# Summing the modulations over partitions inside the preceding stage, with GpSimd held back until the norm is over

## The chip, the cores and the metric

One core of one Trainium2 chip runs the whole program. The metric is device time in microseconds (us) of one execution. Three runs of the kernel before gave 4388.53, 4393.25 and 4394.18 us; the median is 4393.25.

## The reference, cut to what matters

Two transformer blocks of different make, each two layers deep, act on x (256 tokens, width 1024, fp32). In order there are ten sections, each with its own adaptive norm in front and gate behind:

```python
for l in range(2):                                  # first block: sections 0 to 5
    m = (silu(c) @ w_mod[l] + b_mod[l]).reshape(3, 3, D)
    x = x + 0.5 * m[0, 2] * swiglu(adaln_in(x, norm_g[l, 0], m, 0), ...)       # ffn, width 2752
    x = x + m[1, 2] * (mix(adaln_in(x, norm_g[l, 1], m, 1) @ w_in[l]) @ w_out[l])  # attention + conv
    x = x + 0.5 * m[2, 2] * swiglu(adaln_in(x, norm_g[l, 2], m, 2), ...)
for l in range(2):                                  # second block: sections 6 to 9
    sh_m, sc_m, g_m, sh_f, sc_f, g_f = split(silu(c_2) @ w_mod_2[l] + b_mod_2[l], 6)
    x = x + g_m * mixer(rms_norm(x, g) * (1 + sc_m) + sh_m, ...)               # three branches
    x = x + g_f * moe_ffn(rms_norm(x, g) * (1 + sc_f) + sh_f, ...)             # 64 experts, top 8
# adaln_in(x, g, m, i) = rmsnorm(x, g) * (1 + m[i, 1]) + m[i, 0]
```

A section needs a modulation of three vectors of 1024: shift, scale and gate. Each is a vector times a 1024 x 1024 part of `w_mod`. It depends on c alone, not on x, so it can be made at any time ahead.

## The kernel before, in words

The five engines run five hand-written streams, ordered by semaphores. x and h are kept transposed, as 8 tiles of 128 channels x 256 tokens. The sections are, by number: 0 ffn, 1 mixer "ab", 2 ffn, 3 ffn, 4 mixer "cd", 5 ffn, 6 "mix2", 7 moe, 8 "mix2", 9 moe. "Norm s" below is the norm in front of section s.

**Sections.** An ffn or moe section (`units`) goes through units of 256 hidden columns: 1 rest unit and 10 full ones for ffn, 1 shared expert and 64 experts for moe. Each product is three fp32r matmuls, for which ACT makes the rounded half of each weight (`split_up`, `split_down`) and DVE the remainder (`lo_up`, `lo_down`); DVE also makes the hidden values (`hidden`). The units run in a loop of `two_units`, and the last pair stands behind the loop. In a moe section the router (L1017 on TensorE, L1902 on DVE) comes first; its gates are turned by TensorE (`turn_gates`, L1027, L1030) and copied by DVE (L1946, `gates_turned`). A mixer section projects h (`linear`, L802), does attention and convolutions with much small work on DVE, and ends with four output projections and the addition to x (L1549). `next_halves` prepares the first weight halves of the next ffn during the tail of a mixer.

**The norm.** ACT squares x (L1117); TensorE adds the squares over partitions with eight matmuls against ones (L712, bank 2); ACT takes the root (L1124) and DVE the reciprocal (L1518). DVE makes h = x * gain * rstd for eight tiles (L1525); ACT adds the shift (`h_ready`). For ffn, DVE makes the remainder h_lo after each (`lo_h`, L1545), and TensorE's first product waits for each h_lo; for mixers it waits for each h; in moe the router waits for all eight.

**The modulation.** GpSimd (`section`, L601) multiplies 24 row blocks of `w_mod` by c and adds them up into `macc`, 128 partitions x 3072: for each block a scaling (L619; L617 for the first of a third), an addition (L621) and the DMA for the block after next (L604). 24 matmuls with one moving column (L722, fp32, 48 records in the profile) add `macc` over partitions and write 24 columns in PSUM. They are issued in `norm`, directly behind the sum of squares. The first 16 (shift and scale) go to bank 3, the last 8 (gate) to bank 1. DVE waits for the first 16 behind its reciprocal (L1519), adds the bias (L1520) and makes the gain (L1521); it takes the gate's columns after its seventh h (L1529 to L1532). `macc` is single: GpSimd starts the modulation of section s + 1 once the 24 matmuls of norm s are done. Its first two blocks are loaded ahead of that wait. The first modulation is made apart, by DVE and GpSimd during setup.

Of the kernel before, what the change touches and what calls it, by code (L numbers as in the profile page):

```python
# [29 lines left out]
ALU = mybir.AluOpType  # L30
# [158 lines left out]
def build(nc, A, out):  # L189
    ctx = ExitStack()  # L190
    with ctx:
# [404 lines left out]
        @block.gpsimd  # L596
        def _(pool):
            wm1 = A["w_mod"].rearrange("l (p k) m -> l k p m", p=P)
            wm2 = A["w_mod_2"].rearrange("l (p k) m -> l k p m", p=P)

            def section(w, cond0, l, i, s):  # L601

                def fetch(n):
                    pool.dma_start(wmod[:, n % 2, :], w[l][n % KD][:, bass.ds(i * MODS + (n // KD) * D, D)]).then_inc(mod_full[n % 2], 16)  # L604

                fetch(0)
                fetch(1)
                pool.wait_ge(mod_summed, s * 2 + 2)
                for n in range(3 * KD):
                    third, k = n // KD, n % KD  # L610
                    acc = macc[:, third * D:(third + 1) * D]
                    w_n = wmod[:, n % 2, :]
                    c = cond[:, cond0 + k:cond0 + k + 1]
                    pool.wait_ge(mod_full[n % 2], s * (16 * 12) + 16 * (n // 2 + 1))
                    pool.sem_inc(mod_seen, 1)
                    if k == 0:
                        pool.tensor_scalar(acc, w_n, c, 1.0, ALU.mult, ALU.mult).then_inc(mod_step, 1)  # L617
                    else:
                        pool.tensor_scalar(w_n, w_n, c, 1.0, ALU.mult, ALU.mult).then_inc(mod_scaled, 1)  # L619
                        pool.wait_ge(mod_scaled, s * (3 * KD - 3) + (n - third))  # L620
                        pool.tensor_tensor(acc, acc, w_n, ALU.add).then_inc(mod_step, 1)  # L621

                    pool.wait_ge(mod_step, s * (3 * KD) + (n + 1))
                    if n + 2 < 3 * KD:
                        fetch(n + 2)


            pool.wait_ge(cond_done, 2)
            for k in range(KD):
                slot, count, _ = gate_slabs[k // 2]  # L630
                pool.wait_ge(full[slot], count)
                w, acc, c = down_slab(slot)[:, k % 2, :], macc[:, 2 * D:3 * D], cond[:, k:k + 1]
                if k == 0:
                    pool.tensor_scalar(acc, w, c, 1.0, ALU.mult, ALU.mult).then_inc(first_gate, 1)
                else:
                    pool.tensor_scalar(wmod[:, k % 2, :], w, c, 1.0, ALU.mult, ALU.mult).then_inc(gate_scaled, 1)
                    pool.wait_ge(gate_scaled, k)
                    pool.wait_ge(first_gate, k)
                    pool.tensor_tensor(acc, acc, wmod[:, k % 2, :], ALU.add).then_inc(first_gate, 1)
            pool.wait_ge(first_gate, KD)  # L640
            with pool.Fori(0, min(2, SECTIONS)) as i:
                section(wm1, 0, 0, i + 1, i)
            if SECTIONS > 3:
                with pool.Fori(0, 3) as i:
                    section(wm1, 0, 1, i, i + 2)
            if SECTIONS > 6:
                with pool.Fori(0, min(DEPTH, (SECTIONS - 5) // 2)) as l:
                    with pool.Fori(0, 2) as i:
                        section(wm2, KD, l, i, l * 2 + i + 5)
            pool.wait_ge(mod_summed, 2 * SECTIONS)  # L650


        @block.tensor
        def _(pe):
# [53 lines left out]
            def norm(s):  # L708

                for k in range(KD):  # L710
                    pe.wait_ge(sq_done, KD * s + k + 1)
                    ins = pe.matmul(bank[2][:, 0:T], M["ones"], sq[:, k, :], start=(k == 0), stop=(k == KD - 1))  # L712
                ins.then_inc(ms_done, 1)

                if s == 0:
                    pe.wait_ge(first_mod, KD)
                    pe.wait_ge(first_gate, KD)
                    pe.wait_ge(columns_done, len(GROUPS))
                else:
                    pe.wait_ge(mod_step, 3 * KD * s)  # L720
                for j in range(MODT):
                    ins = pe.matmul(bank[3 if j < 2 * KD else 1][:, j:j + 1], macc[:, j * P:(j + 1) * P], M["ones"][:, 0:1], start=True, stop=True)  # L722
                    if j in (2 * KD - 1, MODT - 1):
                        ins.then_inc(mod_summed, 1)

            def three(o, w_hi, w_lo, x_hi, x_lo, start, stop):

# [27 lines left out]
            def units(sec, X):  # L755

                s, slabs, t0, n, moe = sec["s"], sec["slabs"], sec["tile0"], sec["units"], sec["kind"] == "moe"
                rows = P if moe else REST_T
                slot, odd, even = ([q[0] for q in slabs[v]] for v in range(3))
                if t0:  # L760
                    pe.wait_ge(hid_done, t0)
                up(slot, 0, lambda j: sec["half0"] + 1 + j, rows, ready=sec["split0"])
                up(slot, 1, lambda j: up_count(sec, 0, j, 1), rows)
                if moe:
                    turn_gates(X)
                down(slot[2], 0, down_count(sec, 0, 0), t0 + 1, rows, first=True)
                up(odd, 0, lambda j: up_count(sec, 6, j, 0))
                down(slot[2], 1, down_count(sec, 0, 1), t0 + 2, rows)

                def two_units(i, last):  # L770


                    tile, u6 = i * 4 + (t0 + 2), i * 12
                    pe.wait_ge(hid_done, tile)
                    up(odd, 1, lambda j: up_count(sec, u6 + 6, j, 1))
                    down(odd[2], 0, down_count(sec, u6 + 6, 0), tile + 1)
                    up(even, 0, lambda j: up_count(sec, u6 + 12, j, 0))
                    down(odd[2], 1, down_count(sec, u6 + 6, 1), tile + 2)
                    up(even, 1, lambda j: up_count(sec, u6 + 12, j, 1))
                    down(even[2], 0, down_count(sec, u6 + 12, 0), tile + 3)  # L780
                    if not last:
                        up(odd, 0, lambda j: up_count(sec, u6 + 18, j, 0))
                    down(even[2], 1, down_count(sec, u6 + 12, 1, last), tile + 4)

                with pe.Fori(0, n // 2 - 1) as i:
                    two_units(i, False)
                two_units(n // 2 - 1, True)

            def linear(slab, j, taken0, by_token=False, ready=None, halves=(0, 1), heads=None):
# [45 lines left out]
            def mixer1(sec, X):  # L835
# [47 lines left out]
                if sec["kind"] == "cd":  # L883
                    long_conv(X, taken0)
                pe.wait_ge(*X("o_taken", 4))
                pe.wait_ge(*X("conv", CT))
                for c in range(4):
                    linear(slabs[9 + c], 9 + c, taken0, heads=att)
# [22 lines left out]
            def mixer2(sec, X):  # L911
# [87 lines left out]
                for br_, (ready, count, src) in enumerate((("suba", 4, ya), ("lnd", 1 + CT, glu), ("o_taken", 8, yc))):  # L999
                    pe.wait_ge(*X(ready, count))  # L1000
                    for half in range(2):
# [3 lines left out]
                        for m in range(4):  # L1005
# [4 lines left out]
                                ins = pe.matmul(bank[4 + j % 4][:, (m % 2) * T:(m % 2 + 1) * T], w[:, k, m * P:(m + 1) * P], src[:, k, :], start=(k == 0), stop=(k == CT - 1))  # L1010
                            if m % 2:
                                ins.then_inc(proj_done, 1)
                pe.wait_ge(*X("merged", 1))
                for c in range(4):
                    linear(slabs[34 + c], 40 + c, taken0)
# [18 lines left out]
            pe.wait_ge(f_kf, 4)  # L1034
            for sec, X in zip(plan, XS):
                norm(sec["s"])
                if sec["kind"] == "moe":
                    router(sec, X)
                if sec["kind"] in ("ffn", "moe"):
# [356 lines left out]
        def _(dve):  # L1396
            steps = [0]

            def then(ins):

                steps[0] += 1
                ins.then_inc(dve_step, 1)
                dve.wait_ge(dve_step, steps[0])
# [96 lines left out]
            def norm(sec):  # L1500
# [13 lines left out]
                m = modc[:, s % 2, :]  # L1514
                if sec["kind"] in ("ffn", "moe") and s and not sec["early"]:
                    first_halves(sec)
                dve.wait_ge(std_done, s + 1)
                dve.reciprocal(rstd[:, :], std[:, :]).then_inc(rstd_done, 1)  # L1518
                dve.wait_ge(mod_summed, 2 * s + 1)  # L1519
                then(dve.tensor_tensor(m[:, 0:2 * KD], bank[3][:, 0:2 * KD], vec[:, bg, ba:ba + 2 * KD], ALU.add))  # L1520
                then(dve.scalar_tensor_tensor(out=gain[:, s % 2, :], in0=m[:, KD:2 * KD], scalar=1.0, in1=vec[:, gg, ga + row * KD:ga + (row + 1) * KD],  # L1521
                                              op0=ALU.add, op1=ALU.mult))
                dve.wait_ge(rstd_done, s + 1)
                for k in range(KD):
                    dve.scalar_tensor_tensor(out=h[:, k, :], in0=x[:, k, :], scalar=gain[:, s % 2, k:k + 1], in1=rstd[:, :], op0=ALU.mult, op1=ALU.mult).then_inc(scaled_done, 1)  # L1525
                    if sec["kind"] == "ffn" and k:
                        lo_h(sec, k - 1)
                    if k == KD - 2:
                        dve.wait_ge(mod_summed, 2 * s + 2)  # L1529
                        then(dve.tensor_tensor(m[:, 2 * KD:], bank[1][:, 2 * KD:MODT], vec[:, bg, ba + 2 * KD:ba + MODT], ALU.add))  # L1530
                        if s < 6 and s % 3 != 1:
                            then(dve.tensor_scalar(m[:, 2 * KD:], m[:, 2 * KD:], 0.5, None, ALU.mult))  # L1532
                if sec["kind"] == "ffn":
                    lo_h(sec, KD - 1)

# [453 lines left out]
```

## Time and profile before

| what | value |
|---|---|
| median of 3 runs | 4393.25 us (4388.53 to 4394.18) |
| profiled execution, first to last instruction (span) | 4386.6 us |
| PE busy | 4127.6 us, 94% |
| DVE busy | 2587.6 us, 59% |
| ACT busy | 1470.3 us, 34% |
| POOL (GpSimd) busy | 990.2 us, 23% |
| L722, all ten sums | 480 records |
| POOL L617 waiting for PE L722 | 1752.9 us in 9 waits |
| mean granted TensorE clock | 0.965 of 2.4 GHz |

The profile gives the execution's span; no other time of that execution is recorded. Busy times overlap and are averages over stages with different limits. The 1752.9 us are GpSimd waiting for its turn, mostly in the two moe sections, and cost nothing by themselves. Clock shares are of 2.4 GHz: 1.00 is 2.4 GHz, 0.50 is 1.2 GHz.

### The profile page before, as it was taken

How to read it: one execution, taken by the hardware profiler on the slowest of the kernel's cores; microseconds unless marked ns; L12 is line 12 of the kernel's file. 1: busy time of each engine (PE TensorE's matmuls, PEld its weight loads, DVE VectorE, ACT ScalarE, POOL GpSimd, SP SyncE). 2: the span in 40 equal slices, each digit the busy share in tenths (PEclk: the TensorE clock that was granted, in tenths of full speed). 3: DMA queues.
4: the chain of work that ended last, by engine and by line, in shares of the span. 5: the costliest groups of instructions: out<-in, count | busy, mean ns of one | idle time of the engine just before them, and what ended most of it. 6: DMA issues, size and time to landing. Idle time of an engine off the chain costs nothing.

```text
span 4386.6 us, 74944 instructions
## 1 busy us (share of the span) xinstructions
PE 4127.6 (94%) x29877; PEld 3940.1 (90%) x29877; DVE 2587.6 (59%) x3637; ACT 1470.3 (34%) x2008; POOL 990.2 (23%) x640
## 2 busy tenths in 40 slices
PE   4998998987999888999999999998899999999999
PEld 2996898975998777999999999987789999999999
DVE  6754576655755645855555555547345555555555
ACT  1332333321331132333333333311323333333333
POOL 3827465552737104500000000061000000000000
PEclk9999898998999998999999999999989999999999
DMA  6765575752766324765656556563235565565654
GB/s 239 245 197 177 176 248 187 238 187 76 242 222 211 125 83 138 257 194 185 191 191 188 190 189 190 192 219 115 85 118 182 189 196 184 189 194 185 190 192 140
DMA packets 569485, 804.84 MB, mean 183 GB/s; under 512 B 20973, under 2 KB 487860, under 8 KB 568100
## 3 DMA queue, kind: packets, MB, share of 16 engines
q1 hardware_dynamic: 514364, 665.69, 47.2%
q0 software_dynamic: 31104, 113.26, 7.9%
q10 hardware_dynamic: 23912, 24.44, 1.7%
q8 instruction: 72, 1.18, 0.1%
q14 instruction: 33, 0.27, 0.0%
HBM read 802.13 MB, written 1.20 MB: 183 GB/s over the span
## 4 chain that ended last, share of the span: by engine, by line
PE 87%; DVE 10%; ACT 1%; issue 1%; DMA 1%; SPq 0%; ACTq 0%; DVEq 0%
PE bank L728 23%; PE bank L729 23%; PE bank L730 23%; PE bank L802 9%; DVE work L1785 3%; PE bank L1010 2%; PE bank L722 1%; DVE pb L1696 1%; PE bank L712 1%; DMA ring<-in_w_mod 0%; DVE h L1525 0%; PE bank L996 0%; DVE work L1639 0%; DMA ring<-in_ffn_w 0%; PE bank L824 0%
## 5 line engine op out<-in xcount | busy, mean ns | idle before, releaser
L728 PE MATMUL bank<-hh,hi 128*128 128x256 f32 (+1 forms) x5568 | 1588.5, 285 | 32.2 <-DVE h_lo L1545 30.1
L729 PE MATMUL bank<-h_lo,hi 128*128 128x256 f32 (+1 forms) x5568 | 1585.0, 285 | 0.0
L730 PE MATMUL bank<-hh,ring_lo 128*128 128x256 f32 (+1 forms) x5568 | 1584.7, 285 | 0.0
L728 PEld LDWEIGHTS bank<-hh,hi 128*128 128x128 f32 (+1 forms) x5568 | 1073.3, 193 | 38.6 <-DVE h_lo L1545 24.2
L729 PEld LDWEIGHTS bank<-h_lo,hi 128*128 128x128 f32 (+1 forms) x5568 | 1074.3, 193 | 0.0
L730 PEld LDWEIGHTS bank<-hh,ring_lo 128*128 128x128 f32 (+1 forms) x5568 | 1073.9, 193 | 0.0
L1556 DVE TENSOR_TENSOR ring_lo<-ring,hi 128x1024 fp32r<-128x1024 f32 (+1 forms) x696 | 861.1, 1278 | 76.8 <-ACT hi L1141 76.7
L728 PE MATMUL bank<-hid,hi 128*128 128x256 f32 (+1 forms) x2784 | 789.0, 283 | 3.3 <-DVE hid_lo L1588 3.3
L729 PE MATMUL bank<-hid_lo,hi 128*128 128x256 f32 (+1 forms) x2784 | 788.7, 283 | 0.0
L730 PE MATMUL bank<-hid,ring_lo 128*128 128x256 f32 (+1 forms) x2784 | 788.6, 283 | 0.0
L1141 ACT ACTIVATE hi<-ring 128x1024 fp32r<-128x1024 f32 (+1 forms) x696 | 693.1, 1044 | 210.7 <-DMA ring<-in_ws 102.7
L1165 ACT ACTIVATE pb<-bank 128x256 f32<-128x256 f32 (+1 forms) x348 | 133.6, 384 | 1636.1 <-PE bank L730 1608.8
L1580 DVE TENSOR_TENSOR pT<-bank,work 128x256 f32<-128x256 f32 x256 | 108.7, 425 | 860.9 <-ACT pb L1165 860.9
L802 PE MATMUL bank<-h,ring 128*128 128x256 f32 x2432 | 545.7, 384 | 3.9 <-DVE h L1894 3.9
L728 PEld LDWEIGHTS bank<-hid,hi 128*128 128x128 f32 (+1 forms) x2784 | 535.4, 192 | 4.0 <-DVE hid_lo L1588 4.0
L729 PEld LDWEIGHTS bank<-hid_lo,hi 128*128 128x128 f32 (+1 forms) x2784 | 535.5, 192 | 0.0
L730 PEld LDWEIGHTS bank<-hid,ring_lo 128*128 128x128 f32 (+1 forms) x2784 | 535.4, 192 | 0.0
L802 PEld LDWEIGHTS bank<-h,ring 128*128 128x128 f32 x2432 | 468.9, 193 | 73.0 <-DVE h L1894 4.7
L621 POOL TENSOR_TENSOR macc<-macc,wmod 128x1024 f32<-128x1024 f32 x189 | 500.9, 2650 | 15.8
L1560 DVE TENSOR_TENSOR ring_lo<-ring,hi 128x1024 fp32r<-128x1024 f32 (+1 forms) x348 | 476.3, 1369 | 32.7 <-ACT hi L1148 30.6
L1148 ACT ACTIVATE hi<-ring 128x1024 fp32r<-128x1024 f32 (+1 forms) x348 | 368.9, 1060 | 224.5 <-PE bank L730 205.3
L617 POOL TENSOR_SCALAR macc<-wmod,cond 128x1024 f32<-128x1024 f32 x27 | 42.3, 1568 | 1758.2 <-PE bank L722 1752.9
(255 smaller groups left out, 3046.6 us busy)
## 6 DMA issues: line engine op xcount, KB each, us to landing
ring<-in_w SPq DMA_DIRECT2D x384, 1024.0 KB, 5.7
ring<-in_ffn_w SPq DMA_DIRECT2D x120, 1024.0 KB, 6.5
wmod<-in_w_mod POOLq DMA_DIRECT2D x216, 512.0 KB, 4.5
ring<-in_w_in SPq DMA_DIRECT2D x74, 1024.0 KB, 5.4
ring<-in_w_out SPq DMA_DIRECT2D x16, 1024.0 KB, 5.1
work<-gates_scratch ACTq DMA_DIRECT2D x128, 128.0 KB, 5.2
ring<-in_w_mod SPq DMA_DIRECT2D x12, 1024.0 KB, 14.5
ring<-in_ffn_w SPq DMA_DIRECT2D x12, 768.0 KB, 4.8
```

The lines of the kernel that those rows point to most:

```text
L621: pool.tensor_tensor(acc, acc, w_n, ALU.add).then_inc(mod_step, 1)
L728: pe.matmul(o, w_hi, x_hi, start=start, stop=False, skip_group_check=True)
L729: pe.matmul(o, w_hi, x_lo, start=False, stop=False, skip_group_check=True)
L730: return pe.matmul(o, w_lo, x_hi, start=False, stop=stop, skip_group_check=True)
L802: ins = pe.matmul(o[:, half * T:(half + 1) * T], l_, r_, start=(k == 0), stop=(k == KD - 1))
L1141: act.activation(up_hi(j, t, m), up_half(slots[j], t, m), ACT.Copy).then_inc(hi_done, 1)
L1148: act.activation(down_hi(t, rows), down_half(slot, t, rows), ACT.Copy).then_inc(hi_done, 1)
L1165: act.activation(silu[0:m, t, :], bank[t][0:m, 0:T], ACT.Silu).then_inc(silu_done, 1)
L1556: dve.tensor_tensor(up_half(slots[j], t, m, ring_lo), up_half(slots[j], t, m), up_hi(j, t, m), ALU.subtract).then_inc(lo_done, 1)
L1560: dve.tensor_tensor(down_half(slot, t, rows, ring_lo), down_half(slot, t, rows), down_hi(t, rows), ALU.subtract).then_inc(lo_done, 1)
L1580: dve.tensor_tensor(gated[:, t, :], h3, gate, ALU.mult).then_inc(gated_done, 1)
L1785: ins = dve.scalar_tensor_tensor(out=glu[:, t, shift:T], in0=g_in[:, t, 0:T - shift], scalar=w, in1=glu[:, t, shift:T], op0=ALU.mult, op1= ...
```

## The change

The sum over partitions of the modulation of section s + 1 leaves norm s + 1. TensorE does it in section s: before the last pair of units of an ffn or moe section, before the wait for `conv` ahead of the output projection of mixers "ab" and "cd", and before the wait for `merged` in "mix2". The sum for section 0 stays behind norm 0. All 24 columns go to bank 3 and one semaphore step tells of them.

DVE adds the bias and makes gain and gate for all 24 columns ahead of its wait for the root, in front of the reciprocal.

GpSimd begins the modulation n only when the sum before it is done, norm n - 1 has delivered all of h (`h_ready`), and, in a moe section, the gates have been turned. Its loops over sections are written out.

```diff
 # GpSimd
-                pool.wait_ge(mod_summed, s * 2 + 2)
+                pool.wait_ge(mod_summed, n)
+                pool.wait_ge(h_ready, KD * n)
+                if plan[n - 1]["kind"] == "moe":
+                    pool.wait_ge(gates_turned, (n - 1 - 6) // 2 + 1)
...
-            with pool.Fori(0, min(2, SECTIONS)) as i:
-                section(wm1, 0, 0, i + 1, i)
...
+            for n in range(1, SECTIONS):
+                if n < 6:
+                    section(wm1, 0, n // 3, n % 3, n)
+                else:
+                    section(wm2, KD, (n - 6) // 2, n % 2, n)
 # TensorE
-                if s == 0:
+            def sum_mods(n):
+                if n == SECTIONS:
+                    return
+                if n == 0:
                     pe.wait_ge(first_mod, KD)
                     pe.wait_ge(first_gate, KD)
                     pe.wait_ge(columns_done, len(GROUPS))
                 else:
-                    pe.wait_ge(mod_step, 3 * KD * s)
+                    pe.wait_ge(mod_step, 3 * KD * n)
                 for j in range(MODT):
-                    ins = pe.matmul(bank[3 if j < 2 * KD else 1][:, j:j + 1], macc[:, j * P:(j + 1) * P], M["ones"][:, 0:1], start=True, stop=True)
-                    if j in (2 * KD - 1, MODT - 1):
-                        ins.then_inc(mod_summed, 1)
+                    ins = pe.matmul(bank[3][:, j:j + 1], macc[:, j * P:(j + 1) * P], M["ones"][:, 0:1], start=True, stop=True)
+                ins.then_inc(mod_summed, 1)
...
                 with pe.Fori(0, n // 2 - 1) as i:
                     two_units(i, False)
+                sum_mods(s + 1)
                 two_units(n // 2 - 1, True)
...
                 pe.wait_ge(*X("o_taken", 4))
+                sum_mods(s + 1)
                 pe.wait_ge(*X("conv", CT))
...
+                sum_mods(s + 1)
                 pe.wait_ge(*X("merged", 1))
 # VectorE, norm
+                dve.wait_ge(mod_summed, s + 1)
+                then(dve.tensor_tensor(m[:, :], bank[3][:, 0:MODT], vec[:, bg, ba:ba + MODT], ALU.add))
+                if s < 6 and s % 3 != 1:
+                    then(dve.tensor_scalar(m[:, 2 * KD:], m[:, 2 * KD:], 0.5, None, ALU.mult))
+                then(dve.scalar_tensor_tensor(out=gain[:, s % 2, :], ...))
                 dve.wait_ge(std_done, s + 1)
                 dve.reciprocal(rstd[:, :], std[:, :]).then_inc(rstd_done, 1)
...
-                    if k == KD - 2:
-                        dve.wait_ge(mod_summed, 2 * s + 2)
-                        then(dve.tensor_tensor(m[:, 2 * KD:], bank[1][:, 2 * KD:MODT], ...))
```

## Rows read from the trace of the kernel before

**Rows 1.** The page: busy time of TensorE; chain that ended last, shares by engine.
```profile
PE 4127.6 (94%) x29877; PEld 3940.1 (90%) x29877; DVE 2587.6 (59%) x3637; ACT 1470.3 (34%) x2008; POOL 990.2 (23%) x640
...
PE 87%; DVE 10%; ACT 1%; issue 1%; DMA 1%; SPq 0%; ACTq 0%; DVEq 0%
```
**Rows 2.** Stretch of section 2: length, busy PE PEld DVE ACT POOL, clock, DMA share, GB/s.
```profile
640.00:681.00 41.00, 41.00 (x344) 41.00 (x343) 17.60 (x25) 13.34 (x17) 0.00 (x0) 1.00 0.34 107
```
**Rows 3.** Timeline of PE, sums of norms 1 and 8: start, us, what, idle before.
```profile
312.49 7.66 PE L722 MATMUL bank<-mats,macc 128*128 128x1 f32 x48
...
2856.21 5.42 PE L722 MATMUL bank<-mats,macc 128*128 128x1 f32 x48
```
**Rows 4.** Stretches as in rows 2, behind norms 8, 2 and 3.
```profile
2861.70:2865.10 3.40, 3.40 (x9) 2.69 (x9) 2.79 (x6) 2.63 (x7) 2.43 (x3) 0.51 0.02 5
...
479.10:496.20 17.10, 13.97 (x64) 13.17 (x64) 10.94 (x20) 5.25 (x9) 9.76 (x7) 0.50 0.35 113
...
690.80:714.70 23.90, 11.31 (x45) 9.15 (x46) 19.96 (x22) 5.24 (x9) 18.26 (x14) 0.50 0.48 156
```
**Rows 5.** Timeline of DVE and PE in norms 1 and 8.
```profile
313.26 1.75 DVE L1518 RECIPROCAL rstd<-std 128x256 f32<-128x256 f32 x1 [7.54 <-ACT std L1124]
...
320.00 4.61 PE L802 MATMUL bank<-h,ring 128*128 128x256 f32 x10
...
2856.91 1.75 DVE L1518 RECIPROCAL rstd<-std 128x256 f32<-128x256 f32 x1 [2.03 <-ACT std L1124]
```
**Rows 6.** Timeline of DVE and POOL in norm 2.
```profile
477.15 1.75 DVE L1518 RECIPROCAL rstd<-std 128x256 f32<-128x256 f32 x1 [2.02 <-ACT std L1124]
...
482.31 0.48 DVE L1545 SCALAR_TENSOR_TENSOR h_lo<-h,modc,hh 128x256 fp32r<-128x256 f32 x1 [0.18 <-ACT hh L1129]
...
488.58 2.64 DVE L1525 SCALAR_TENSOR_TENSOR h<-x,gain,rstd 128x256 f32<-128x256 f32 x1
...
491.79 0.48 DVE L1545 SCALAR_TENSOR_TENSOR h_lo<-h,modc,hh 128x256 fp32r<-128x256 f32 x1 [0.18 <-ACT hh L1129]
...
488.60 2.34 POOL L621 TENSOR_TENSOR macc<-macc,wmod 128x1024 f32<-128x1024 f32 x1
```
**Rows 7.** Timeline of DVE in norm 3.
```profile
690.79 1.74 DVE L1518 RECIPROCAL rstd<-std 128x256 f32<-128x256 f32 x1
...
709.69 1.57 DVE L1545 SCALAR_TENSOR_TENSOR h_lo<-h,modc,hh 128x256 fp32r<-128x256 f32 x1 [0.18 <-ACT hh L1129]
```
**Rows 8.** Timeline of sections 7 and 9; last row: waits in section 7, us, times, longest.
```profile
1701.15 7.06 PE L1024 MATMUL bank<-wr,h 128*128 128x64 f32 x32 [4.29 <-ACT h L1133]
...
3240.44 7.06 PE L1024 MATMUL bank<-wr,h 128*128 128x64 f32 x32 [4.30 <-ACT h L1133]
...
2851.66 3.23 DVE L1549 SCALAR_TENSOR_TENSOR x<-bank,modc,x 128x256 f32<-128x256 f32 x8 [3.66 <-PE bank L730]
...
4376.34 3.23 DVE L1549 SCALAR_TENSOR_TENSOR x<-bank,modc,x 128x256 f32<-128x256 f32 x8 [3.67 <-PE bank L730]
...
PEld bank L1030 <- DVE pb L1942: 10.4, 1, 10.4
```
**Rows 9.** Timeline of PE before the output projections of sections 1, 6; a stretch of section 1.
```profile
441.54 3.68 PE L802 MATMUL bank<-work,ring 128*128 128x256 f32 x8 [0.73 <-ACT work L1263]
...
1657.47 6.74 PE L802 MATMUL bank<-h,ring 128*128 128x256 f32 x30 [1.96 <-DVE h L1894]
...
431.40:445.00 13.60, 9.84 (x24) 6.64 (x25) 9.40 (x24) 1.58 (x3) 1.13 (x2) 0.50 0.23 78
```
**Rows 10.** Stretches of L1785 alone (length, DVE busy, clock); POOL's last additions, sections 1, 2.
```profile
1422.00:1441.00 19.00, 19.00 (x20) 1.00 0.73 240
1441.00:1460.00 19.00, 19.00 (x50) 1.00 0.58 190
...
428.64 2.34 POOL L621 TENSOR_TENSOR macc<-macc,wmod 128x1024 f32<-128x1024 f32 x1
...
623.16 3.25 POOL L621 TENSOR_TENSOR macc<-macc,wmod 128x1024 f32<-128x1024 f32 x1
```

More of the change, by code:

```diff
@@ L599, in _, with section, fetch @@
             wm2 = A["w_mod_2"].rearrange("l (p k) m -> l k p m", p=P)
-            def section(w, cond0, l, i, s):
-                def fetch(n):
-                    pool.dma_start(wmod[:, n % 2, :], w[l][n % KD][:, bass.ds(i * MODS + (n // KD) * D, D)]).then_inc(mod_full[n % 2], 16)
+            def section(w, cond0, l, i, n):
+                def fetch(j):
+                    pool.dma_start(wmod[:, j % 2, :], w[l][j % KD][:, bass.ds(i * MODS + (j // KD) * D, D)]).then_inc(mod_full[j % 2], 16)
@@ L606, in section @@
                 fetch(0)
                 fetch(1)
-                pool.wait_ge(mod_summed, s * 2 + 2)
-                for n in range(3 * KD):
-                    third, k = n // KD, n % KD
+                pool.wait_ge(mod_summed, n)
+                pool.wait_ge(h_ready, KD * n)
+                if plan[n - 1]["kind"] == "moe":
+                    pool.wait_ge(gates_turned, (n - 1 - 6) // 2 + 1)
+                for j in range(3 * KD):
+                    third, k = j // KD, j % KD
                     acc = macc[:, third * D:(third + 1) * D]
-                    w_n = wmod[:, n % 2, :]
+                    w_j = wmod[:, j % 2, :]
@@ L613, in section @@
                     c = cond[:, cond0 + k:cond0 + k + 1]
-                    pool.wait_ge(mod_full[n % 2], s * (16 * 12) + 16 * (n // 2 + 1))
+                    pool.wait_ge(mod_full[j % 2], (n - 1) * (16 * 12) + 16 * (j // 2 + 1))
                     pool.sem_inc(mod_seen, 1)
                     if k == 0:
-                        pool.tensor_scalar(acc, w_n, c, 1.0, ALU.mult, ALU.mult).then_inc(mod_step, 1)
+                        pool.tensor_scalar(acc, w_j, c, 1.0, ALU.mult, ALU.mult).then_inc(mod_step, 1)
@@ L618, in section @@
                     else:
[L619 to L625, printed above, removed]
+                        pool.tensor_scalar(w_j, w_j, c, 1.0, ALU.mult, ALU.mult).then_inc(mod_scaled, 1)
@@ L628, in _ @@
+                        pool.wait_ge(mod_scaled, (n - 1) * (3 * KD - 3) + (j - third))
+                        pool.tensor_tensor(acc, acc, w_j, ALU.add).then_inc(mod_step, 1)
+                    pool.wait_ge(mod_step, (n - 1) * (3 * KD) + (j + 1))
+                    if j + 2 < 3 * KD:
+                        fetch(j + 2)
             pool.wait_ge(cond_done, 2)
@@ L640, in _ @@
             pool.wait_ge(first_gate, KD)
-            with pool.Fori(0, min(2, SECTIONS)) as i:
-                section(wm1, 0, 0, i + 1, i)
[L643 to L650, printed above, removed]
+            for n in range(1, SECTIONS):
[3 more added lines that the diff above has]
+                    section(wm2, KD, (n - 6) // 2, n % 2, n)
+            pool.wait_ge(mod_summed, SECTIONS)
         @block.tensor
@@ L1036, in _ @@
                 norm(sec["s"])
+                if sec["s"] == 0:
+                    sum_mods(0)
                 if sec["kind"] == "moe":
@@ L1516, in norm @@
                     first_halves(sec)
+                dve.wait_ge(mod_summed, s + 1)
+                then(dve.tensor_tensor(m[:, :], bank[3][:, 0:MODT], vec[:, bg, ba:ba + MODT], ALU.add))
+                if s < 6 and s % 3 != 1:
+                    then(dve.tensor_scalar(m[:, 2 * KD:], m[:, 2 * KD:], 0.5, None, ALU.mult))
+                then(dve.scalar_tensor_tensor(out=gain[:, s % 2, :], in0=m[:, KD:2 * KD], scalar=1.0, in1=vec[:, gg, ga + row * KD:ga + (row + 1) * KD],
+                                              op0=ALU.add, op1=ALU.mult))
                 dve.wait_ge(std_done, s + 1)
                 dve.reciprocal(rstd[:, :], std[:, :]).then_inc(rstd_done, 1)
[L1519 to L1522, printed above, removed]
                 dve.wait_ge(rstd_done, s + 1)
@@ L1527, in norm @@
                         lo_h(sec, k - 1)
-                    if k == KD - 2:
-                        dve.wait_ge(mod_summed, 2 * s + 2)
-                        then(dve.tensor_tensor(m[:, 2 * KD:], bank[1][:, 2 * KD:MODT], vec[:, bg, ba + 2 * KD:ba + MODT], ALU.add))
-                        if s < 6 and s % 3 != 1:
-                            then(dve.tensor_scalar(m[:, 2 * KD:], m[:, 2 * KD:], 0.5, None, ALU.mult))
                 if sec["kind"] == "ffn":
```

## The prediction

> **What bounds the kernel now.** I read the page first: engine times and the chain of work that ended last [rows 1]. TensorE is busy 94% of the span and makes 87% of the chain; VectorE makes 10%. Inside the ffn and moe stages nothing else counts: from 640 to 681 us, the last two units of section 2, PE is busy for all 41 us at full clock while DVE is busy for 17.6 [rows 2]. Any PE work put there is paid in full. The slack lies elsewhere, and for that I read the timelines of the ten norms, where PE waits for DVE, then the router, then the places in the mixers where PE waits before the output projection.
>
> The sum over partitions is 24 fp32 matmuls with one moving column, 48 records. In norm 8 it takes 5.42 us [rows 3], which is 0.113 us a record at full clock. The reader is to see what the clock does next: PE had no pause, yet between 2861.7 and 2865.1 the granted clock is 0.51, the 1.2 GHz level, and PE was doing dense projection work in that stretch [rows 4]. All ten norms show such a fall, 2 to 5 us after the first one-column matmul; three of the low stretches stand in [rows 4]. In norm 1, where the clock was low for part of it, the sum took 7.66 us [rows 3].
>
> **What the change removes: the sum from the norms.** Norm 0 keeps it.
> Norms 1, 4, 6, 8 (mixers follow). In norm 1 the reciprocal ends at 315.01 [rows 5]. Without the wait for the sum, the first h (0.48), its shift on ACT (about 0.5) and a semaphore step put the first projection matmul at 316.05; it was at 320.00 [rows 5]: 3.9 us. In norm 8 the reciprocal ends at 2858.66 [rows 5], so PE can start at 2859.7 against the sum's end at 2861.6 [rows 3]: 1.8. Norm 6 repeats norm 8 (1.8), norm 4 lies between (its sum ran partly at low clock; 2.8). Together 10.3.
> Norms 2, 3, 5, 0 (ffn follows). PE is paced here by pairs of h and h_lo, one of each (0.48 us, the next starting just before the end) every 0.79 us. In norm 2 the reciprocal ends at 478.90, so the first h_lo can start at 480.0 and end at 480.5, and the eighth is done at 486.0. It was done at 492.27 [rows 6]: 6.2 us. Two causes are in that: the sum (2 us), and GpSimd, which begins in the middle of the norm. The last h took 2.64 us instead of 0.48, exactly beside GpSimd's 2.34 us addition (488.58 and 488.60 [rows 6]), with the gate's small operations queued in front. The added gate operations (0.6 us) move ahead of the reciprocal; in norm 2 they are hidden behind the wait for std, in norms 0 and 3 not. Norm 3: reciprocal ends 692.53, plus 0.6, plus 7.1 gives 700.2 against 711.26 [rows 7]: 11.0. Norms 5 and 0, two more of norm 2's pattern, give 6.6 and 5.8 by the same working. Together 29.6.
> Norms 7 and 9 (moe): all eight h are made before the router's matmuls; DVE waited 2.4 us for the sum (here at low clock), so 2.7 each, 5.4.
> Bounds: nothing beyond the wait for the sum is won if GpSimd was innocent (about 20), the whole 45.3 if both causes hold. I take 45.
>
> **What the later start of GpSimd removes: the router of section 7.** Sections 7 and 9 are the same work; GpSimd runs beside the router in 7 and has nothing left in 9. From the first router matmul to the addition to x at the end it is 1701.15 to 2851.66 in section 7 and 3240.44 to 4376.34 in section 9 [rows 8]: 1150.5 against 1135.9, 14.6 us. The difference arises in the router: in section 7 PE waits 10.4 us for DVE's gates [rows 8], in section 9 not at all, as DVE's many small operations meet no GpSimd there. After the change GpSimd starts once the gates are turned: 14.6 us go. Bounds: 0, if something else makes the difference, and 14.6.
>
> **The clock in the norms.** Where PE starts dense work late and at 1.2 GHz, it loses half of that stretch. After norm 2 the clock is low until 496.2, after norm 3 until 714.7 [rows 4], 3.9 and 3.4 us after the eighth h_lo; norms 5 and 0 have 5.0 and 2.7, and the four mixer norms between 3.4 and 5.5. That is 32 us, a loss of 16. With the one-column matmuls gone the idle time is shorter, but not gone (3.3 us in norm 8): I expect to keep 5 of these 16 and win 11. Bounds: 0 and 16.
> Removed in all: 45 + 14.6 + 11 = 71.
>
> **What the change adds: nine sums inside sections.** Five fall before the last two units of ffn or moe sections (0, 2, 3, 5, 7). PE has no slack there [rows 2], DVE and ACT have, so the full price counts: 5.4 us at full clock, plus what the clock takes. One low stretch of 3.4 us as in norm 8 costs 1.7 of dense work; norm 4's was twice as long. I take 3.0, so 8.4 each, 42 in all. Below: 5.4 each (no fall), 27. Above: the whole sum at half clock, 9.6 (48 times 0.2), and 1.7 after it, 11.3 each, 56.
> Three stand where PE waits about 2 us before the output projection of sections 4, 6 and 8 (1.96 for the last merge product in section 6 [rows 9]). That cover hides 1.9: 6.5 each, 19.5 (below 3.5 each, above 9.4 each).
> Section 1 has no cover: PE starts the projection at 441.54, 0.73 us of idle after its last matmul, and the clock is low from 431.4 to 445 [rows 9]. The sum runs at half clock and keeps it low: 9.8 (below 5.4, above 11.3).
> Added: 71.3, between 43 and 96.
>
> **What GpSimd's later start adds.** In the mixers DVE is on the path, and GpSimd is now active some 2.5 us longer relative to it. The taps of section 6 show the price: 20 in 19 us beside GpSimd, 50 in 19 us after it [rows 10], so 0.6 us lost per us. Four mixers: 5 to 6 us; I take 5 (below 0, above 8). In the ffn and moe sections the shift is covered: GpSimd's last addition for section 2's successor ends at 626 [rows 10], the last two units begin at about 653 (28.8 us before the end, from their matmuls at 0.12 us each), and it moves by about 7 us; section 0 has some 13 us left, 3 and 5 more. The tight one is section 1: its last addition ends at 430.98 [rows 10]; about 1.5 us earlier now, while PE arrives at its sum about 5 us earlier, near 436. Six us are left, so the wait costs nothing; if GpSimd were slower by more than that, PE would wait for the difference. The loops on GpSimd are written out: same steps, static addresses, 0.
>
> **Sum.** Against the profiled execution (span 4386.6; the median of the runs shown, 4393.25, lies 6.7 above it, taken as fixed): minus 71, plus 71.3, plus 5: about plus 5. Predicted 4398. A measurement of this kernel tells about 0.2%, 9 us, from no change, so this is no measurable change. The gains and losses are each 16 times larger than their difference, which is why the range is wide.
>
> **The rule that would change the sum.** Rows 3 and 4 show the clock falling while PE is busy without a pause in one-column matmuls. The Trainium skill, "TensorE: Matmul & The Clock Gate", Part 1, says that the gate is set by how busy the engine has recently been. Taken at its word, back-to-back matmuls would keep 2.4 GHz. This case's trace does not agree for one-column matmuls: 0.51 was granted directly behind them.
>
> **Rivals.**
> (A) With dense matmuls on both sides the sum does not lower the clock. For: in the norms there was also idle time near each fall, before or after. Against: in norm 8 it fell with PE busy throughout. Then eight sums cost 3.0 less and section 1's 4.4 less: 4398 - 28 = 4370, faster. That is the time the skill's rule above leads to. 0.15.
> (B) Slower: the clock falls early in each in-section sum, so that nearly all of it runs at 1.2 GHz and dense work behind it too. Place: before the last two units and the output projections. Price 11.3 instead of 8.4, 9 times: plus 25, 4423. For: norm 1's 7.66 us, and sections 7 and 9, where most of the sum was at low clock. Against: norms 6 and 8 ran it in 5.4. It decides from about 9 us per sum on, where the total passes plus 9. 0.23.
> (C) The router of section 7 is not relieved, since GpSimd was not its cause or still runs beside it: plus 14.6, 4413. Section 9 speaks against it. 0.05.
> (D) GpSimd is late for section 1 or for an ffn section and PE waits there: some 10 us, 4408. Against: the margins above. 0.04.
> (E) More is won in the norms than I count, as the waits of DVE, ACT and PE are chained: all upper bounds give 4383. 0.06.
>
> **From the cases to the numbers.** My forecast has 0.47; its own spread is about 10 us, so 0.05 of it lies beyond plus 9 and a little beyond minus 9. Faster: A, E and 0.01: 0.20. Slower: B, part of C and D, and the edge of the forecast: 0.34. Same: 0.46. Range: 4376 to 4418; it leaves out the far half of A and of B.
>
> **What would show it.** In the profile after: the line of the sum matmuls inside sections, 48 records at 5.4 to 9.6 us, with a granted clock of 0.5 beside or just behind each (A wrong, B or the forecast right by length). In norm 2 the eighth h_lo about 9 us after the end of the norm's own matmuls instead of 15.7. In section 7 no DVE operation of the router above 0.5 us, and from the first router matmul to the x addition about 1136 plus the 8.4 of its own sum. PE waiting on GpSimd nowhere. I am wrong if PE stays at full clock behind the sums, or if the norms shrink by much less than 45.

## The result, and the profile after

The changed kernel takes 4403.57 us (median of 8 runs, 4395.53 to 4410.78), the kernel before 4392.97 us (8 runs, 4382.86 to 4397.58). The ratio is 1.003, with a 95% interval of 1.002 to 1.0041: slower by 0.2 to 0.4%, 10.6 us by the medians. The forecast was 4398, in a range of 4376 to 4418.

The profiled execution has a span of 4393.7 us, against 4386.6. The page after, in the lines that answer to [rows 1]:

```profile
PE 4130.1 (94%) x29877; PEld 3942.4 (90%) x29877; DVE 2583.7 (59%) x3627; ACT 1469.7 (33%) x2008; POOL 1010.0 (23%) x640
...
PE 86%; DVE 10%; ACT 2%; issue 1%; DMA 1%; SPq 0%; DVEq 0%; ACTq 0%
```

The page tells little: each share moved by a point at most. The stages tell more. This table is worked out from the timelines, as the time from one section's first addition to x to the next one's (the rows of L1549 before, L1554 after), in us; e3 and e4 are experiments below.

```
section            0      1      2      3      4      5      6      7       8      9
before         300.1  171.8  209.8  218.7  194.7  210.7  372.9  1172.9  366.5  1158.2
after           -6.0   +4.3   +2.3   -4.2   +4.1   -2.0   +8.3    -4.8   +7.5    -3.0
e4, hold only   -6.7   +2.4   -6.0  -10.8   +7.4   -7.0   +3.1    -7.4   +0.6    -1.4
e3, one column  -8.2   -0.2   -7.8  -12.4   -0.1   -8.7   +1.7    -9.7   +2.7    -2.7
```

(Section 0 holds the setup, which took 6.5 us less in this one profile and as long as before in the next, e1: chance.) Sections 6 and 8 lose 8 us each, 1 and 4 lose 4 each, 3 and 7 win 4 to 5. Each row is one profile; section 4 came out 4.1 us longer here and 10.1 in e1, which is the same kernel, so a mixer's row is good to some us only.

**The norms did what was forecast.** Timeline of DVE in norm 2, after; it answers to [rows 6]:

```profile
475.55 1.75 DVE L1532 RECIPROCAL rstd<-std 128x256 f32<-128x256 f32 x1 [1.60 <-ACT std L1132]
477.33 0.88 DVE L1535 SCALAR_TENSOR_TENSOR h<-x,gain,rstd 128x256 f32<-128x256 f32 x2
478.39 0.48 DVE L1550 SCALAR_TENSOR_TENSOR h_lo<-h,modc,hh 128x256 fp32r<-128x256 f32 x1 [0.18 <-ACT hh L1137]
...
483.82 0.48 DVE L1550 SCALAR_TENSOR_TENSOR h_lo<-h,modc,hh 128x256 fp32r<-128x256 f32 x1 [0.18 <-ACT hh L1137]
```

The h follow the reciprocal without a gap. The eighth h_lo ends 7.0 us after the reciprocal; before it was 13.4 (478.90 to 492.27). Counted from the end of the norm's own matmuls it is 9.4 us, where the prediction said about 9 and before it was 15.7. The clock falls there are shorter too: 10.2 us of low clock in and behind norm 3 instead of 23.9.

**The router is relieved.** Section 7 after, answering to [rows 8]; the first row of PE starts at the first router matmul (one record is missing from the trace):

```profile
1705.49 6.84 PE L1030 MATMUL bank<-wr,h 128*128 128x64 f32 x31 [9.66 <-ACT h L1141]
...
2853.80 2.44 DVE L1554 SCALAR_TENSOR_TENSOR x<-bank,modc,x 128x256 f32<-128x256 f32 x6 [3.66 <-PE bank L733]
```

That is 1148.3 us instead of 1150.5: 2.2 less, with a sum of its own in it. The forecast was about 1144; before, section 9, which holds no sum, took 1135.9. So about 4 us of the relief were not kept (e9 shows where they went).

**The sums inside sections.** Timeline of PE: the sum in section 2, in section 1 and in section 6, then stretches (length, busy PE PEld DVE ACT POOL, clock, DMA share, GB/s) behind the first and the last:

```profile
643.31 8.26 PE L726 MATMUL bank<-mats,macc 128*128 128x1 f32 x48
...
428.94 10.40 PE L726 MATMUL bank<-mats,macc 128*128 128x1 f32 x48 [0.47 <-ACT work L1271]
...
1657.55 5.59 PE L726 MATMUL bank<-mats,macc 128*128 128x1 f32 x48
1663.00 2.48 PE L806 MATMUL bank<-h,ring 128*128 128x256 f32 x5
```
```profile
645.50:655.70 10.20, 10.20 (x49) 10.20 (x50) 0.32 (x1) 0.00 (x0) 0.00 (x0) 0.50 0.24 96
...
1662.60:1666.00 3.40, 3.40 (x11) 2.86 (x11) 1.23 (x1) 1.06 (x1) 0.00 (x0) 0.51 0.00 0
```

The clock fell to 1.2 GHz 2.2 us into the sum of section 2, in the middle of a stage that had run at 2.4 GHz for 160 us, and PE was busy without a pause from 640 us to the end of the low stretch. In section 1 the clock was low already, from 420.2 us on. The projection in section 6 starts at 1663.00, 5.3 us behind the last merge matmul, where it was 2.0 [rows 9].

### The profile page after: what moved, and what is told of

The parts are those of the page before. It is cut to its first block, busy times and chain, and to the rows that moved or that the text cites. A ratio compares the mean times of both kernels' runs of the same rounds, so it can differ in the third digit from the quotient of the medians.

```text
span 4393.7 us, 73959 instructions
## 1 busy us (share of the span) xinstructions
PE 4130.1 (94%) x29877; PEld 3942.4 (90%) x29877; DVE 2583.7 (59%) x3627; ACT 1469.7 (33%) x2008; POOL 1010.0 (23%) x640
## 4 chain that ended last, share of the span: by engine, by line
PE 86%; DVE 10%; ACT 2%; issue 1%; DMA 1%; SPq 0%; DVEq 0%; ACTq 0%
PE bank L731 22%; PE bank L732 22%; PE bank L733 22%; PE bank L806 10%; DVE work L1790 2%; PE bank L1015 2%; PE bank L726 2%; PE bank L712 1%; DVE pb L1701 1%; PE bank L1001 0%; DMA ring<-in_w_mod 0%; DVE hid L1591 0%; DVE ring_lo L1565 0%; PE bank L828 0%; DVE work L1654 0%
## 5 line engine op out<-in xcount | busy, mean ns | idle before, releaser
L1561 DVE TENSOR_TENSOR ring_lo<-ring,hi 128x1024 fp32r<-128x1024 f32 (+1 forms) x696 | 877.3, 1301 | 99.1 <-ACT hi L1149 99.1
L1565 DVE TENSOR_TENSOR ring_lo<-ring,hi 128x1024 fp32r<-128x1024 f32 (+1 forms) x348 | 476.6, 1370 | 32.2 <-ACT hi L1156 30.8
```

The source lines that it names most:

```text
L1561: dve.tensor_tensor(up_half(slots[j], t, m, ring_lo), up_half(slots[j], t, m), up_hi(j, t, m), ALU.subtract).then_inc(lo_done, 1)
L1565: dve.tensor_tensor(down_half(slot, t, rows, ring_lo), down_half(slot, t, rows), down_hi(t, rows), ALU.subtract).then_inc(lo_done, 1)
```

## The experiments

Each was timed against the kernel before on the same chip; "changed" is the changed kernel, 4403.88 us as e1 has it. e1 to e4 ran on one chip, e5 to e8 on a second, e9 and e10 on a third; the kernel before took 4392.09, 4392.55 and 4388.54 us there. A difference between two of them carries the error of both, some 8 to 13 us.

**e1, the changed kernel again.** 

> The changed kernel once more, on the chip of the three kernels beside it. About 10 us above the kernel before (4403 beside 4393). If the setup before norm 0 was shorter by 6.5 us only by chance in the first profile, this profile shows a setup as long as before within a few us.

Measured: 4403.88, ratio 1.0026 (1.0011 to 1.0041). The setup was 88.9 us long to the end of norm 0's matmuls (before 89.3, first profile after 82.8). Its gain was chance; the change costs 11 us.

**e2, the same work in dense matmuls.**
```diff
-                for j in range(MODT):
+                if n:
+                    for j in range(MODS // T):
+                        ins = pe.matmul(bank[3][:, (j % 2) * T:(j % 2 + 1) * T], M["ones"], macc[:, j * T:(j + 1) * T], start=True, stop=True)
+                for j in range(0 if n else MODT):
                     ins = pe.matmul(bank[3][:, j:j + 1], macc[:, j * P:(j + 1) * P], M["ones"][:, 0:1], start=True, stop=True)
```


> Sums 1 to 9 are replaced by 12 fp32 matmuls of 256 columns each over the same macc, so the modulations are wrong from section 1 on; the PE time at full clock is about the same (24 records of 0.23 us, 5.6 us, against 5.4 to 5.6). Theory (the one-column matmuls lower the granted clock, and that costs 2 to 3 us each on top): 18 to 27 us faster than the changed kernel, 4376 to 4386, and no low clock behind the sums in sections 0, 2, 3, 5 and 7. Rival (the clock has its dips anyway, the sums cost their own PE time only): within 5 us of the changed kernel, 4400.

Measured: 4376.44, ratio 0.9969 (0.9957 to 0.9981), 27.4 below the changed kernel, 3.0 for each of nine. The stretch around the sum of section 2:

```profile
640.00:655.00 15.00, 15.00 (x109) 14.38 (x108) 4.67 (x6) 3.33 (x4) 0.00 (x0) 1.00 0.29 100
```

PE is as busy as before and the clock stays at 2.4 GHz. No low stretch begins in any of the nine sums or within 25 us behind it; each takes 5.35 us, and 6.1 in section 1, where the clock was low already. The theory holds, and the rival falls: matmuls with one moving column lowered the clock. The rate of weight loads hardly tells the two apart: 343 in 41 us of dense work at 2.4 GHz [rows 2], and 46 in the first 5.0 us of the sum in section 5 of the changed kernel, behind which the clock fell.

**e3, one column of 24.**
```diff
-                for j in range(MODT):
+                for j in range(1 if n else MODT):
```


> Sums 1 to 9 do one of their 24 matmuls, so 23 of 24 columns are not made (the modulations are wrong). It takes nearly all of the in-section price away. Theory: the price was about 71 us in all, so 4332. Rival (price 5.4 us each, less 2 us of cover in three mixers): 43 us, so 4360.

Measured: 4343.73, ratio 0.9889 (0.9866 to 0.9912), 60 below the changed kernel. So nine sums cost 60 us by the medians, 6.7 each: between theory (71) and rival (43). The intervals of the two ratios leave some 12 us either way, so 71 is not excluded and 43 is. With e2, 27 of the 60 are the clock.

**e4, the other half of the change alone.** GpSimd of the changed kernel on the TensorE and VectorE of the kernel before:
```diff
-                pool.wait_ge(mod_summed, s * 2 + 2)
+                pool.wait_ge(mod_summed, 2 * n)
+                pool.wait_ge(h_ready, KD * n)
+                if plan[n - 1]["kind"] == "moe":
+                    pool.wait_ge(gates_turned, (n - 1 - 6) // 2 + 1)
```


> The kernel before with GpSimd's new waits and written-out loops; the sums stay in the norms. Theory: GpSimd's part of the norms of sections 0, 2, 3 and 5 (about 18 us) with some low clock (3), and the router of section 7 (14.6) go; GpSimd beside the mixers' chains (5) and beside the first experts (4) comes: 4393 - 27 = 4366. Rival (the norms were limited by the sum, GpSimd was innocent): 4393 - 15 + 9 = 4387 from the router alone.

Measured: 4359.01, ratio 0.9926 (0.9905 to 0.9946), 33 below the kernel before and 45 below the changed one, and 7 below what even the theory expected. GpSimd was not innocent. In norm 3, where it started at the very first h, the eighth h_lo comes 13.7 us after the sum of squares with the sum still in the norm; that is what the changed kernel reaches (13.7) and 11.1 less than before. Norm 2 is at 11.4, between 15.7 and the changed kernel's 9.4. The last sum of squares and the eighth h_lo of norm 3 in e4:

```profile
672.36 3.72 PE L712 MATMUL bank<-pb,mats 128*128 128x256 f32 x16 [1.02 <-ACT pb L1117]
...
689.34 0.48 DVE L1545 SCALAR_TENSOR_TENSOR h_lo<-h,modc,hh 128x256 fp32r<-128x256 f32 x1 [0.18 <-ACT hh L1129]
```

**e5, GpSimd beside the router again.**
```diff
-                if plan[n - 1]["kind"] == "moe":
-                    pool.wait_ge(gates_turned, (n - 1 - 6) // 2 + 1)
```


> The changed kernel without the one wait for the turned gates: GpSimd runs beside the router of section 7 again. Theory: the router's 14.6 us and some low clock (17 in all) come back and the 5 to 7 us of TensorE waits in the first experts partly go: 4403 + 10 to 12 = 4414, and the section from the sum of squares to the addition to x is some 10 us longer than in the changed kernel's profile. Rival (the router's slowness had another cause): 4403 or less.

Measured: 4416.33, ratio 1.0062 (1.0043 to 1.0081); section 7 is 16 us longer than in the changed kernel. As expected by the theory; this one wait is worth 12 us by the medians, each against the kernel before on its own chip.

**e6, the sums moved, GpSimd not held at all** (both waits taken out of the changed kernel). 

> The changed kernel without both new waits of GpSimd: it starts each modulation right behind the sum inside the preceding section, some 35 us earlier. Theory: the four ffn norms have GpSimd beside them again (plus 18) and the router too (plus 15), while in the mixers GpSimd ends earlier relative to their chains (minus 12 at least, minus 25 with the taps of sections 6 and 8 free of it): 4403 + 33 - 20 = about 4416. Rival (what counts is only how long GpSimd overlaps with anything, the total being unchanged): 4403.

Measured: 4422.86, ratio 1.0076 (1.0046 to 1.0105); above the theory's 4416 and far from the rival. Sections 2 and 3 are 13 and 14 us longer than before and section 7 is 10 longer, section 8 is 9 shorter, while GpSimd's busy time is much the same (968 us for 1010): which work GpSimd runs beside decides.

**e7, e8, e10, e9: what a better version needs.** e7 keeps GpSimd held and sums in the norm, with six columns (`EARLY`) ahead of the sum of squares; `columns_of` issues the matmuls of the columns it is given:
```diff
+                early = EARLY if s else 0
+                if s:
+                    pe.wait_ge(mod_step, 3 * KD * s)
+                    columns_of(range(early))
                 for k in range(KD):
                     pe.wait_ge(sq_done, KD * s + k + 1)
...
+                columns_of(range(early, MODT))
```


> Held GpSimd as in e4, sums in the norms, but 6 of the 24 columns are summed ahead of the sum of squares, in the 1.0 us in which TensorE waits for x, and 18 behind. The result is complete. Theory: the wait for the first 16 columns, up to 1.8 us a norm, mostly goes, and TensorE is free about when the first h is there: 9 times 1.0 to 1.5 us less than e4's 4359, so 4348. Rival (the early columns only delay the sum of squares by what they save): 4359.

Measured: 4344.74, ratio 0.9893 (0.9871 to 0.9914), 14 below e4: the theory (4348). In norms 4 to 6 the first h comes 1.3 us earlier than in e4 (2.6 us behind the sum of squares for 3.9).

e8 adds two edits to GpSimd, e10 only the first of them, e9 puts the second alone into the changed kernel. The second paces GpSimd: beside a moe section it does one of its 24 blocks per expert.
```diff
-                pool.wait_ge(h_ready, KD * n)
+                if plan[n - 1]["kind"] in ("ffn", "moe"):            # e8, e10
+                    pool.wait_ge(h_ready, KD * n)
...
                 for j in range(3 * KD):
+                    if plan[n - 1]["kind"] == "moe":                 # e8, e9
+                        pool.wait_ge(down_done, plan[n - 1]["tile0"] + 2 * (j + 1))
```


> e7 with two more edits: before the mixers' norms GpSimd is not held (its overlap with the mixers' chains costs 0.6 us per us), and in section 7 it does one of its 24 blocks per expert instead of running without a pause, so that DVE is not saturated. The result is complete. Theory: minus 5 to 7 us in section 7, minus 6 to 10 in the four mixers: 4335. Rival (the mixers' longer times come from the clock, not from GpSimd): only section 7's part, 4342.

> e8 without the pacing in section 7, so e7 with the one edit that GpSimd is not held before the mixers' norms. The result is complete. Theory: what GpSimd's later start cost the mixers comes back, 2 us and more in each of sections 4, 6 and 8: 4344.7 - 6 = 4339, with section 7 as long as in e7. Rival (e8 won only by section 7): 4345.

> The changed kernel with one edit: in section 7 GpSimd does one of its 24 blocks per expert. Theory (GpSimd without a pause saturates DVE beside the first experts, and TensorE waits 4 to 6 us for hidden values): section 7 is 5 us shorter in the profile and the time 4403 - 5 = 4398. Rival (those waits of TensorE come from its earlier start, DVE's work being late anyway): section 7 unchanged within 1 us, 4403.

Measured: e8 4335.5, ratio 0.9872 (0.985 to 0.9894), the fastest version of the study, 57 us below the kernel before. Its expectation was met in time and not in mechanism, as e10 shows. e10 4345.15, ratio 0.9889 (0.9871 to 0.9908), no faster than e7: the rival was right, holding GpSimd before the mixers' norms costs nothing that can be measured. So what e8 wins comes from the pacing: 7 us (ratios) to 14 (medians) against e10, of which section 7 holds 4.5 in the profiles. e9 4392.58, ratio 1.001 (0.9999 to 1.002): the pacing takes the changed kernel back to the kernel before within the error. The waits of PE behind the router in the changed kernel, then stretches of the changed kernel and of e9 while GpSimd works there:

```profile
PE bank L731 <- DVE hid_lo L1593: 5.1, 5, 2.2
```
```profile
1760.00:1800.00 40.00, 38.73 (x321) 38.33 (x320) 39.60 (x30) 14.32 (x19) 34.36 (x22) 1.00 0.83 280
1800.00:1864.00 64.00, 62.35 (x515) 61.97 (x516) 62.66 (x51) 23.92 (x29) 52.92 (x31) 1.00 0.81 269
```
```profile
1780.00:1820.00 40.00, 40.00 (x336) 40.00 (x335) 27.01 (x34) 15.77 (x19) 15.74 (x8) 1.00 0.63 209
```

In the changed kernel DVE (third pair) is busy 39.60 of 40 us and PE has gaps; with GpSimd paced it is busy 27.01 and PE has none. Section 7 of e9 is 4.9 us shorter, as forecast. In e8, held and paced, section 7 takes 1144.8 us from the norm's last sum of squares to the first addition to x, and section 9, which has no GpSimd beside it, 1144.7 (before: 1162.8 and 1148.2): GpSimd was the whole difference between the two moe sections. The rest of what e9 wins over the changed kernel (11 us by medians, 7 by the ratios) is not settled; in its profile it stands in section 8 (last section of this document).

## Why the prediction was right

The time (4404 for 4398) and the direction came out. The case named as mine was "no measurable change" within 9 us, and the medians lie 10.6 apart, just beyond. This table sets the terms of the sum beside the two profiles of the changed kernel, in us against the kernel before. "Up to the sum" runs from the norm's last sum of squares to the last matmul ahead of the sum inside the section, "at their place" from there to the addition to x. The forecast's 11 us of clock are split by the low stretches that it lists: 15 us behind the four ffn norms, so 7.5, and the remaining 3.5 for the mixers.

```
                                  forecast   changed      e1
sections 0, 2, 3, 5 up to the sum    -37.1     -35.6   -36.2
section 7 up to its sum              -17.3     -13.4   -13.3
section 9                             -2.7      -3.2    -3.5
mixers up to their sums               -8.8      -1.5    +0.7
nine sums, at their place            +71.3     +67.2   +67.5
together                              +5.4     +13.5   +15.2
```

The setup's 6.5 us of chance are left out. Point by point:

- *Ffn norms, 29.6 us and 7.5 of the clock.* Right, as the first line shows; in e3, which has nearly nothing of the sums in it, these sections are 35.5 us shorter from the sum of squares to the addition to x. Both causes are shown apart by e4.
- *Norms 7 and 9, 2.7 each.* Right: the router's matmuls start 2.7 and 2.6 us earlier behind the sum of squares.
- *Router, 14.6.* Right in mechanism and size at its place: in section 7 PE is 17.6 us ahead at the 300th matmul of the units, the norm's 2.7 among them. Not all was kept: 13.4 are left at the 2000th. "Covered" was wrong here, since GpSimd now runs beside the first experts and PE waits there 5 us for hidden values. With GpSimd paced (e9) PE is 18.1 us ahead at both.
- *The rule on the clock.* The trace decided against the rule taken at its word: e2 has the same busy PE and no fall. The price of 3.0 us a sum that was taken between 1.7 and 3.5 is what e2 measured: 27.4 for nine, good to some 8.
- *Nine sums, 71.3.* Right in mechanism and nearly in size: 67 at their place in both profiles, 60 between whole runs (e3). The five of the ffn and moe sections cost 8.2 and 8.1 each, for 8.4. The one in section 1 took 10.4 us at half clock and cost 10.7 and 10.0, for 9.8. Those of sections 4, 6 and 8 cost 15.7 and 16.8 together, for 19.5.
- *The mixers, 8.8 shorter: 10.3 from their norms and 3.5 of the clock, less 5 for GpSimd's later start.* This is the part that was mis-sized, by 7 and 9.5 us. Why stays open. For the later start as the cause speaks e4, where GpSimd is held and the sums stay: the four mixers are 13.6 us longer than before. Against it speaks e10: not held there, it is no faster than e7, and its mixers are within 1 us as long in all.

Section 6 shows that the start of GpSimd is not all of it. DVE's taps (L1785 before, L1790 after) in the stretch beside GpSimd and behind it; the first pair answers to [rows 10]. Below it stand the stretches from 274 us behind the norm to the last products ahead of the sum, before and after:

```profile
1426.70:1446.00 19.30, 19.30 (x37) 1.00 0.69 225
1446.00:1465.00 19.00, 19.00 (x51) 1.00 0.42 136
```
```profile
1591.00:1632.00 41.00, 30.64 (x123) 25.15 (x123) 14.07 (x26) 11.82 (x14) 0.00 (x0) 0.92 0.19 65
...
1590.00:1634.00 44.00, 33.79 (x121) 27.46 (x122) 13.69 (x25) 11.61 (x14) 0.00 (x0) 0.81 0.17 56
```

The taps began 5.9 us later behind the norm (110.8 us for 104.9) but ran faster (50.7 us for 57.4, three slow ones for eight), so they end 0.8 us ahead: half of PE's 1.5 us from the norm is still there. The section then loses 3.4 us between 274 and 318 us, long after GpSimd's last addition (119 us): nearly the same instructions at a granted clock of 0.81 for 0.92, with 17.1 us at 1.2 GHz for 6.8. The term of 0.6 us per us of overlap could not hold this, and why the low stretch is longer there is not shown.

So the nearness of the number is in part luck: the sums were 4 us too high, and mixers and router together 11 to 14 too low, which offset each other. Apart from that both sides of the balance hold, the sums within 6% and the gains within 21%. Some figures of the prediction are slips that do not move the forecast: the gains and losses are about 14 times their difference, not 16; the chances of "faster" add up to 0.22, not 0.20; the upper bounds with 0 for GpSimd give about 4389, not 4383; and 640 to 681 us holds more than the last two units, which take 28.8.

Of the rivals, A is refuted by the low clock beside dense work on both sides. B's mechanism was met in sections 1 and 2 (10.4 and 8.3 us), but the price over nine was 7.5 on average. C and D did not come: section 7 was relieved, and PE waited nowhere for GpSimd. E did not come.

## What to carry to other kernels

A change that bundles two ideas should be timed as two: here holding GpSimd back was worth minus 33 us, and moving the sums as well plus 45. Before work is moved off a visible wait, ask what covered it where it stood: the sums filled time in which PE could only wait for the root and the reciprocal, and the new place had no idle time. Where GpSimd slows VectorE, as in these taps, it should run where VectorE is not the limit, in portions with pauses between them (e9). And do not expect back-to-back one-column matmuls to keep the clock up: here they lowered it.

## What the runs showed of the hardware

- TensorE in back-to-back 128x1 fp32 matmuls was granted 1.2 GHz after 2 to 5 us in eight sums inside sections (in the ninth the clock was low already); the same time in 128x256 fp32 matmuls left it at 2.4 GHz (e2). Over the nine sums that costs 27 us. One matmul of 128x1 took 0.23 us at 2.4 GHz and 0.43 at 1.2 GHz (24 in 5.41 us in norm 8 before, 24 in 10.40 in section 1).
- GpSimd and VectorE hold each other up, and either can lose. Beside GpSimd's 2.4 us addition, a tap of 0.45 us took 2.6, before and after. In e9 it was the other way round: one scaling of GpSimd, 1.1 us alone, stood for 46 us, as long as VectorE's taps ran back to back without a wait, and no tap was slow. Timeline of GpSimd in section 8 of e9:

```profile
2962.09 3.20 POOL L627 TENSOR_TENSOR macc<-macc,wmod 128x1024 f32<-128x1024 f32 x1
...
2967.79 46.27 POOL L625 TENSOR_SCALAR wmod<-wmod,cond 128x1024 f32<-128x1024 f32 x1 [1.59 <-DMA wmod<-in_w_mod]
```

That section was 8.8 us shorter than in the changed kernel's profile. The long wait of GpSimd was seen in e9 and in e10 (section 6, 45.0 us, one slow tap). What decides which of the two loses was not tested and stays open.
